# First MLP product of blocks 1 to 7 as seven quarter products, weight sums by adding DMAs

## The chip, the cores and the metric

One core of a Trainium2 chip. The time is that of the whole kernel on the device, in microseconds. Three runs of the kernel before took 737.86, 737.99 and 738.38 us; the median is 737.99.

## The reference, cut to what matters

The kernel computes one decoder layer on 512 tokens of 1024 channels, in float32. Two token mixers (a gated linear recurrence and a sparse attention) come first; the change leaves them alone. Then comes the MLP:

```python
        hm = rms_norm(x, mlp_norm_g[l])
        x = x + jnp.square(jax.nn.relu(hm @ w_mlp_in[l])) @ w_mlp_out[l]
    return rms_norm(x, final_norm_g)
```

`w_mlp_in` is 1024 x 4096, `w_mlp_out` 4096 x 1024.

## The kernel before, in words

**Three matmuls for one.** Every float32 operand is split into a rounded part (float32r, "hi") and the remainder ("lo"); a product is hi x hi + hi x lo + lo x hi (`three`, L1518 to L1522). So each weight slab of 128 x 1024 that a DMA loads from `slabs` is rounded by ScalarE (`whi`, four slots) and its remainder taken by VectorE (`wlo`, four slots). `hi_done` and `lo_done` count them.

**The MLP in eight blocks.** A block is 512 hidden features (`FB`). Its first product, `hidden` (L1780), makes four tiles of 128 features x 512 tokens in banks 0 to 3, each from one slab by 8 x 3 matmuls of 512 columns: 96 matmuls. ScalarE applies relu and squares them into `hv`. The second product multiplies `hv` (512 tokens x 512 features) with 512 x 1024 weights. In blocks 0 to 6 this is done by seven products of half the size in each of the three directions instead of eight (Winograd's form of Strassen's scheme): `PRODUCTS` (L69) gives their order, `block_` on TensorE (L1793) does them with 12 matmuls of 512 columns each, 84 in all. It needs sums of the four weight parts (`w_sum` on VectorE, L1375: four per block, from the arrived `br` slabs) and of the four activation parts (`s_sum`, L1383). A product is rounded on ScalarE (`a_hi`, `hi_out`), its remainders are taken on VectorE (`a_lo`, `lo_out`), and VectorE adds the finished product from its two banks to `acc` in SBUF (`gather`, L1394), except for two products that stay in banks 4 to 7 over all blocks (`KEPT`). Block 7, `last_`, does its second product plainly, with 96 matmuls, adds the `acc` slabs to `y` and ends with the last norm.

**What sets the order.** Nothing is scheduled: each engine has its own list, written out by hand (`block_` and `last_` of ScalarE L942, VectorE L1402, TensorE L1793; a hardware loop over the blocks), and waits on counted semaphores. `full[b]` counts what TensorE finished in bank b, `free[b]` what was read out of it. SP issues the loads (`load_out` L517 for the four `br` slabs, L540 for the next block's `raw` slabs), each when `lo_done` says that the slab before it is used. GpSimd does nothing in the loop. In the mixer part it issues 23 DMAs of another kind (`split_by_dma`, L644, L649): an SBUF slab added onto another, `accum_op=ALU.add`, which gives a `wlo` remainder without VectorE.

Of the kernel before, what the change touches and what calls it, by code (L numbers as in the profile page):

```python
# [18 lines left out]
F32 = mybir.dt.float32  # L19
# [49 lines left out]
PRODUCTS = (1, 7, 4, 5, 6, 3, 2)  # L69
# [5 lines left out]
def build(nc, x, slabs, vecs, consts, onehot, rel_bias, final_g, out):  # L75
    with ExitStack() as ctx:
# [6 lines left out]
        def sem(name):  # L83
# [92 lines left out]
        ssg, r2y = small[:, 242:246], small[:, 246:250]  # L176
# [10 lines left out]
        br_in = {k: sem(f"br_in{k}") for k in br}  # L187
        hi_done, lo_done, lod_done, slab_used = sem("hi_done"), sem("lo_done"), [sem(f"lod_done{q}") for q in range(SLOTS)], sem("slab_used")
# [11 lines left out]
                 "rik_done ry_done rf_done fe_done z_done act_fin pool_step acc_zero wt_done s_done ah_done al_done ymix_done mix_step iqh_done aqh_done kdh_done ikh_done ikl_done")  # L200
# [198 lines left out]
        NST = NFB - 1  # L399
        WPB = 4 + len(PRODUCTS)  # L400
        PBANKS = ((0, 1), (4, 5), (2, 3), (0, 1), (2, 3), (0, 1), (6, 7))
        KEPT = (1, 6)
        USE_B = [4, 4, 3, 3]

        def in_use(m, it):

            return it * USE_B[m] + MB

        def out_use(p, q, it):

            b = PBANKS[p][q]
            return it * USE_B[b] + (MB + {0: 1, 3: 2, 5: 3, 2: 1, 4: 2}[p])

        def product_full(p, q, it):

            b = PBANKS[p][q]
            return full[b], it + (MB2[b - 4] + 1) if p in KEPT else out_use(p, q, it) + 1

        def loop_blocks(eng, body, last):

            with eng.Fori(0, NST, 1) as it:
                body(it)
            last(NST)
# [39 lines left out]
        a_src = [a_part(0, 0), two(sa), a_part(1, 1), two(sb), two(sx), two(sa), a_part(0, 1)]  # L463
        w_src = [br["11"], br["12"], wt4, wt1, wt2, br["22"], br["21"]]
        w_last = [br["11"], br["21"], br["12"], br["22"]]
        w_last_in = ["11", "21", "12", "22"]
        hh3 = hh[:, :].rearrange("p (k t) -> p k t", k=4)
# [32 lines left out]
        def _(sp):  # L500
# [13 lines left out]
            def mlp_slab(m, it):  # L514
                return slabs[bass.ds(it * PER_FB + (NPLAN + m), 1), :, :].rearrange("a p c -> (a p) c")

            def load_out(it):  # L517

                for k, m, after in (("11", 4, WPB - 3), ("12", 6, WPB - 5), ("22", 7, WPB - 1), ("21", 5, WPB)):
                    sp.wait_ge(lo_done, it * WPB + (NLO - WPB + after))  # L520
                    sp.dma_start(br[k][:, :], mlp_slab(m, it)).then_inc(br_in[k], 16)
# [8 lines left out]
            sp.wait_ge(S["mxl_done"], KD_)  # L530
            sp.dma_start(fg[:, :], final_g.partition_broadcast(P)).then_inc(fg_in, 16)
# [1403 lines left out]
```

## Time and profile before

| | us |
|---|---|
| median of three runs | 737.99 |
| the profiled execution | 737.4 |
| its span | 735.7 |
| TensorE busy | 718.9 |
| VectorE busy | 513.0 |
| ScalarE busy | 378.4 |
| GpSimd busy | 109.2 |
| first matmul of the MLP starts, from the span's start | 399.4 |
| last matmul of the MLP starts | 728.4 |

The profile shows one execution. TensorE's row "busy" is the time in which at least one matmul is under way; matmuls overlap, so the number of them times the duration of one is more than that. "Idle before" in the table of groups is the time for which an engine stood still before such an instruction, with the work that released it.

### The profile page before, as it was taken

How to read it: one execution, taken by the hardware profiler on the slowest of the kernel's cores; microseconds unless marked ns; L12 is line 12 of the kernel's file. 1: busy time of each engine (PE TensorE's matmuls, PEld its weight loads, DVE VectorE, ACT ScalarE, POOL GpSimd, SP SyncE). 2: the span in 40 equal slices, each digit the busy share in tenths (PEclk: the TensorE clock that was granted, in tenths of full speed). 3: DMA queues.
4: the chain of work that ended last, by engine and by line, in shares of the span. 5: the costliest groups of instructions: out<-in, count | busy, mean ns of one | idle time of the engine just before them, and what ended most of it. 6: DMA issues, size and time to landing. Idle time of an engine off the chain costs nothing.

```text
span 735.7 us, 9813 instructions
## 1 busy us (share of the span) xinstructions
PE 718.9 (98%) x3490; PEld 603.1 (82%) x3490; DVE 513.0 (70%) x791; ACT 378.4 (51%) x595; POOL 109.2 (15%) x145
## 2 busy tenths in 40 slices
PE   5999999999999999999999999999999999999996
PEld 4788878888888888888888888888888888888885
DVE  5686996777896754337435695868778695968964
ACT  6463545867854665543224654545364544545432
POOL 4421241012212456400200100000000000000002
PEclk9999999999999999999999999999999999999999
DMA  8555123644997653112713242241515051332002
GB/s 298 153 99 150 58 90 83 132 117 105 224 221 176 144 119 110 58 58 86 257 58 129 101 142 87 88 141 57 171 36 190 2 171 57 116 113 86 30 1 114
DMA packets 25051, 85.12 MB, mean 116 GB/s; under 512 B 2712, under 2 KB 4920, under 8 KB 25016
## 3 DMA queue, kind: packets, MB, share of 16 engines
q1 hardware_dynamic: 19104, 67.87, 27.5%
q0 software_dynamic: 3312, 12.06, 8.8%
q10 hardware_dynamic: 2600, 4.72, 2.9%
q8 instruction: 22, 0.36, 0.2%
q14 instruction: 13, 0.11, 0.1%
HBM read 68.91 MB, written 3.67 MB: 99 GB/s over the span
## 4 chain that ended last, share of the span: by engine, by line
PE 95%; ACT 2%; DVE 1%; DMA 1%; issue 0%; POOL 0%; SPq 0%; POOLq 0%; DVEq 0%; ACTq 0%
PE bank L1520 20%; PE bank L1522 20%; PE bank L1521 20%; PE bank L1566 9%; PE bank L1570 8%; PE bank L1567 8%; PE bank L1751 2%; PE bank L1528 2%; PE bank L1659 2%; DMA xs<-x 1%; PE bank L1733 1%; PE bank L1732 1%; PE bank L1649 1%; PE bank L1650 1%; PE bank L1710 0%; PE bank L1671 0%
## 5 line engine op out<-in xcount | busy, mean ns | idle before, releaser
L1520 PE MATMUL bank<-hTh,whi 128*128 128x512 f32 (+1 forms) x264 | 102.8, 389 | 0.5 <-DVE hTl L1045 0.5
L1522 PE MATMUL bank<-hTh,wlo 128*128 128x512 f32 (+1 forms) x264 | 102.7, 389 | 0.0
L1521 PE MATMUL bank<-hTl,whi 128*128 128x512 f32 (+1 forms) x264 | 102.7, 389 | 0.0
L683 ACT CAST whi<-raw 128x1024 fp32r<-128x1024 f32 x58 | 60.3, 1041 | 41.3 <-PE bank L1522 40.7
L1566 PE MATMUL bank<-hTh,whi 128*128 128x512 f32 x192 | 78.0, 406 | 1.0 <-DVE hTl L1045 1.0
L1520 PE MATMUL bank<-whi,ah 128*128 128x512 f32 x196 | 76.2, 389 | 0.0
L1521 PE MATMUL bank<-wlo,ah 128*128 128x512 f32 x196 | 76.2, 389 | 0.0
L1522 PE MATMUL bank<-whi,al 128*128 128x512 f32 x196 | 76.2, 389 | 0.0
L1570 PE MATMUL bank<-hTl,whi 128*128 128x512 f32 x192 | 75.1, 391 | 0.0
L1567 PE MATMUL bank<-hTh,wlo 128*128 128x512 f32 x192 | 74.9, 390 | 0.0
L934 ACT ACTIVATE rt<-bank 128x512 f32<-128x512 f32 x32 | 19.1, 598 | 85.8 <-PE bank L1522 85.8
L1019 DVE TENSOR_TENSOR wlo<-raw,whi 128x1024 fp32r<-128x1024 f32 x34 | 45.3, 1334 | 24.6 <-ACT whi L683 24.6
L1520 PEld LDWEIGHTS bank<-hTh,whi 128*128 128x128 f32 (+1 forms) x264 | 49.2, 186 | 11.3 <-issue 0.7
L1521 PEld LDWEIGHTS bank<-hTl,whi 128*128 128x128 f32 (+1 forms) x264 | 49.2, 186 | 10.8
L1522 PEld LDWEIGHTS bank<-hTh,wlo 128*128 128x128 f32 (+1 forms) x264 | 49.2, 186 | 10.6
L925 ACT CAST whi<-raw 128x1024 fp32r<-128x1024 f32 x29 | 29.8, 1052 | 50.3 <-PE bank L1522 50.3
L1367 DVE TENSOR_TENSOR wlo<-br,whi 128x1024 fp32r<-128x1024 f32 x32 | 39.0, 1219 | 18.8 <-ACT whi L930 18.5
L666 POOL TENSOR_SCALAR small<-small 128x1 f32<-128x1 f32 x4 | 0.8, 191 | 310.0 <-ACT junk L702 310.0
L1400 DVE TENSOR_TENSOR acc<-bank,acc 128x512 f32<-128x512 f32 x70 | 44.8, 682 | 0.0
L1521 PEld LDWEIGHTS bank<-wlo,ah 128*128 128x128 f32 x196 | 36.8, 188 | 7.7
L1520 PEld LDWEIGHTS bank<-whi,ah 128*128 128x128 f32 x196 | 36.8, 188 | 7.6
L1522 PEld LDWEIGHTS bank<-whi,al 128*128 128x128 f32 x196 | 36.8, 188 | 7.6
(245 smaller groups left out, 1625.6 us busy)
## 6 DMA issues: line engine op xcount, KB each, us to landing
raw<-slabs SPq DMA_DIRECT2D x87, 512.0 KB, 3.5
br<-slabs SPq DMA_DIRECT2D x32, 512.0 KB, 3.5
wlo<-raw POOLq DMA_DIRECT2D x23, 512.0 KB, 4.9
xs<-x SPq DMA_DIRECT2D x4, 512.0 KB, 5.2
y<-x ACTq DMA_DIRECT2D x1, 2048.0 KB, 8.8
bias_rows<-rbias ACTq DMA_DIRECT2D x1, 1536.0 KB
out<-ys SPq DMA_DIRECT2D x3, 512.0 KB, 2.6
bt<-bias_rows ACTq DMA_DIRECT2D x1, 1024.0 KB, 6.1
```

What stands on the lines that cost most here:

```text
L683: act.copy(whi[s][:, :], raw[s][:, :]).then_inc(hi_done, 1)
L925: act.copy(whi[s][:, :], raw[s][:, :]).then_inc(hi_done, 1)
L934: act.activation(rt[m % 2][:, :], bank[m][:, :], ACT.Relu).then_inc(free[m], 1)
L1019: dve.tensor_tensor(wlo[s][:, :], raw[s][:, :], whi[s][:, :].bitcast(F32), ALU.subtract).then_inc(lo_done, 1)
L1367: dve.tensor_tensor(wlo[s][:, :], src[:, :], whi[s][:, :].bitcast(F32), ALU.subtract).then_inc(lo_done, 1)
L1400: dve.tensor_tensor(a_, bank[b][:, :], a_, ALU.add).then_inc(free[b], 1)
L1520: pe.matmul(dst, lh, rh, start=start, stop=False)
L1521: pe.matmul(dst, lh, rl, start=False, stop=False)
L1522: return pe.matmul(dst, ll, rh, start=False, stop=stop)
L1566: pe.matmul(dst, wh[:, k, c0:c0 + P], hi_[:, k, t0:T], start=k == 0, stop=False)
L1567: pe.matmul(dst, wl[:, k, c0:c0 + P], hi_[:, k, t0:T], start=False, stop=False)
L1570: ins = pe.matmul(dst, wh[:, k, c0:c0 + P], lo_[:, k, t0:T], start=False, stop=k == kt - 1)
```

## The change

It touches the MLP alone.

- The first product of blocks 1 to 7 (`up_product`, L2055) is done as the second one was: seven products over quarters, each 2 x 4 x 3 = 24 matmuls of 256 columns, 168 in all, in banks 3, 2, 3, 2, 3, 0, 3 (`UP_BANK`). Some products are added onto each other in the bank; ScalarE copies products 0, 1 and 2 out (`keep`), VectorE adds them onto products 3, 4 and 5 (`quadrant`), and ScalarE applies relu and the square by quadrant. Block 0 keeps the plain form. The activations' sums (T) are made once: GpSimd adds `hTh + hTl` in eight sums, VectorE makes four sums of 128x1024, ScalarE rounds four, VectorE takes four remainders, all during block 0.
- All weight sums, four for each product, are made by adding DMAs that GpSimd issues (`sums`), from slabs that SP loads: twelve loads a block instead of eight, seven of them (`load_quarter`) in two runs of 512 values per partition. VectorE's `w_sum` is gone.
- The second product has other signs, so that every weight sum is a plain addition, and three `ah` and `al` buffers in turn instead of seven. VectorE now takes 14 weight remainders a block, before 11. Block 0 copies its products to `acc`, where before GpSimd had set them to zero.

The core of the diff, from the file after. GpSimd:

```python
            def sums(it):

                pool.wait_ge(d1_in, it * 16 + 32)
                pool.wait_ge(br_in["22"], it * 16 + 32)
                add_into(d1, br["22"], ds_in[1])
                pool.wait_ge(br_in["12"], it * 16 + 32)
                pool.wait_ge(br_in["11"], it * 16 + 32)
                add_into(br["12"], br["11"], ds_in[3])
                pool.wait_ge(raw_in[ring(0)], raw_count(0, it + 1))
                pool.wait_ge(raw_in[ring(2)], raw_count(2, it + 1))
                add_into(r21, r11, us_in[3])
                pool.wait_ge(sl_in[1], it * 16 + 32)
                pool.wait_ge(raw_in[ring(3)], raw_count(3, it + 1))
                add_into(s1, r22, us_in[1])
                pool.wait_ge(lo_done, NLO + out_op(1, it))
                pool.wait_ge(ds_in[3], it * 16 + 32)
                pool.wait_ge(ds_in[1], it * 16 + 32)
                add_into(br["11"], d1, ds_in[2])
...
                pool.wait_ge(lo_done, NLO + out_op(3, it))
                pool.wait_ge(ds_in[2], it * 16 + 32)
                add_into(br["21"], br["11"], ds_in[4])
```

VectorE, the second half of a block:

```python
            def second_half(it):
                a_lo(3, it)
                lo_out(4, it)
                gather(1, it)
                lo_out(5, it)
                a_lo(4, it)
                gather(2, it)
                lo_out(6, it)
                a_lo(5, it)
                gather(3, it)
                a_lo(6, it)
                gather(4, it)
                lo_up(0, it + 1)
                gather(5, it)
                lo_up(1, it + 1)
                lo_up(2, it + 1)
```

ScalarE, the same half:

```python
            def second_half(it):
                ended(0, it)
                hi_out(4, it)
                a_hi(3, it, "hv_done", 4)
                ended(1, it)
                hi_out(5, it)
```

and SP, which loads the next block's slabs:

```python
            def next_out(it):

                sp.wait_ge(lo_done, NLO + out_op(1, it))
                load_out("12", 6, it + 1)
```

`hi_out(pos)` waits for the DMA or the sum whose slab it rounds: `ds_in[2]` for position 4, `ds_in[4]` for 6, `us_in` for quarter products 1 to 4.

The order of the instructions, on three engines. First VectorE, the second half of the MLP's loop before, from the sum for the fifth product on; `wlo`, `al` are remainders, L1400 is `gather`:

```order
L1392 TENSOR_TENSOR al_148<-sb,ah_141 128x512 [waits ah_done]
...
L1400 TENSOR_TENSOR acc_127<-bank,acc_127 128x512 [waits full0]
...
L1400 TENSOR_TENSOR acc_127<-bank,acc_127 128x512 [waits full1]
...
L1388 TENSOR_TENSOR sa<-hv,sx 128x512 [waits s_done,al_done]
...
L1392 TENSOR_TENSOR al_149<-sx,ah_142 128x512 [waits ah_done]
...
L1367 TENSOR_TENSOR wlo_60<-wt_133,whi_56 128x1024 [waits hi_done]
```

and in the file after, the same part of VectorE's loop (L1576 is the weight remainder, `d_133` the slab `d1`, `br_123` the slab `br11`, L1620 `gather`):

```order
L1589 TENSOR_TENSOR sx<-sb,hv 128x512 [waits s_done]
...
L1576 TENSOR_TENSOR wlo_58<-d_133,whi_54 128x1024 [waits hi_done]
...
L1599 TENSOR_TENSOR al_151<-sb,ah_148 128x512 [waits ah_done]
...
L1589 TENSOR_TENSOR sa<-sx,hv 128x512 [waits s_done,hv_done]
...
L1576 TENSOR_TENSOR wlo_59<-br_125,whi_55 128x1024 [waits hi_done]
...
L1599 TENSOR_TENSOR al_149<-hv,ah_146 128x512 [waits ah_done]
...
L1576 TENSOR_TENSOR wlo_60<-br_123,whi_56 128x1024 [waits hi_done]
...
L1620 TENSOR_TENSOR acc_127<-bank,acc_127 128x512 [waits full0]
```

Before, the first gather stood directly behind the remainders of position 3; now two weight remainders and an activation's stand between the last activation sum and it, and the last of them is that of `br11`.

GpSimd, from the start of the MLP on, in the file after (`hf_132` is hTh + hTl; the eight DMAs repeat for each block):

```order
L759 TENSOR_TENSOR hf_132<-hTh,hTl 128x2x256 [waits free3]
L666 TENSOR_SCALAR small<-small 128x4 [waits sq_done]
L667 TENSOR_TENSOR small<-small 128x4 [waits pool_step]
L765 TENSOR_TENSOR small<-small 128x4 [waits pool_step]
L766 TENSOR_SCALAR small<-small 128x4 [waits pool_step]
L769 DMA d_133<-br_126 128x1024 [waits br_in22,d1_in]
L769 DMA br_124<-br_123 128x1024 [waits br_in11,br_in12]
L769 DMA raw_50<-raw_52 128x1024 [waits raw_in1,raw_in3]
L769 DMA s_134<-raw_51 128x1024 [waits raw_in2,sl_in1]
L769 DMA br_123<-d_133 128x1024 [waits ds_in1,ds_in3,lo_done]
```

Before, GpSimd had five memsets and three small sums here and nothing in the loop.

ScalarE in block 0, in the file after (L1060 rounds a weight slab, L1087 a sum T, L1083 an activation):

```order
L1083 ACTIVATE ah_146<-hv 128x512 [waits hv_done]
L1060 CAST whi_53<-br_124 128x1024 [waits ds_in3]
L1087 ACTIVATE th_137<-hf_132 128x1024 [waits ts_done]
L1087 ACTIVATE th_138<-hf_132 128x1024 [waits ts_done]
L1087 ACTIVATE th_139<-hf_132 128x1024 [waits ts_done]
L1114 ACTIVATE rt_120<-bank 128x512 [waits full2]
L1116 ACTIVATE hv<-rt_120 128x512 [waits free2]
L1060 CAST whi_54<-d_133 128x1024 [waits ds_in1]
```

The relus of the third and fourth hidden tile, which before waited for their bank alone, now stand behind the rounding of `br_124` (`br12`), which waits for its adding DMA.

## Rows read from the trace of the kernel before

**Rows 1.** The page: busy us (share of the span) by engine; the chain that ended last

```profile
PE 718.9 (98%) x3490; PEld 603.1 (82%) x3490; DVE 513.0 (70%) x791; ACT 378.4 (51%) x595; POOL 109.2 (15%) x145
...
PE 95%; ACT 2%; DVE 1%; DMA 1%; issue 0%; POOL 0%; SPq 0%; POOLq 0%; DVEq 0%; ACTq 0%
```

**Rows 2.** Timeline of TensorE in the MLP: start us, us, engine, line, operation

```profile
455.05 0.39 PE L1522 MATMUL bank<-hTh,wlo 128*128 128x512 f32 x1
...
459.81 0.39 PE L1522 MATMUL bank<-hTh,wlo 128*128 128x512 f32 x1
```

**Rows 3.** Timeline of TensorE, the narrow products of the indexer

```profile
135.63 0.28 PE L1649 MATMUL bank<-ikh,iqs 128*128 128x256 f32 x1
...
136.11 0.40 PE L1520 MATMUL bank<-whi,hTh 128*128 128x512 f32 x1
```

**Rows 4.** Timeline around two 128-column products: weight loads and matmuls

```profile
233.48 0.19 PEld L1566 LDWEIGHTS bank<-oah,whi 128*128 128x128 f32 x1
...
233.59 0.19 PEld L1567 LDWEIGHTS bank<-oah,wlo 128*128 128x128 f32 x1
```

**Rows 5.** Groups of instructions, 480 to 680 us: busy us, mean ns, idle before

```profile
L1400 DVE TENSOR_TENSOR acc<-bank,acc 128x512 f32<-128x512 f32 x47 | 30.1, 682 | 0.0
...
L1367 DVE TENSOR_TENSOR wlo<-br,whi 128x1024 fp32r<-128x1024 f32 x20 | 24.4, 1219 | 15.5 <-ACT whi L930 15.5
...
L930 ACT CAST whi<-br 128x1024 fp32r<-128x1024 f32 x20 | 20.9, 1046 | 6.1 <-PE bank L1522 6.1
...
L936 ACT ACTIVATE hv<-rt 128x512 f32<-128x512 f32 x20 | 12.6, 632 | 0.6
L934 ACT ACTIVATE rt<-bank 128x512 f32<-128x512 f32 x20 | 12.0, 598 | 58.3 <-PE bank L1522 58.3
...
L940 ACT ACTIVATE ah<-hv 128x512 fp32r<-128x512 f32 x15 | 9.4, 625 | 0.0
L1392 DVE TENSOR_TENSOR al<-sa,ah 128x512 fp32r<-128x512 f32 x10 | 6.9, 688 | 8.2 <-ACT ah L940 8.2
```

**Rows 6.** Timeline of VectorE in one stretch without waits

```profile
469.19 0.68 DVE L1392 TENSOR_TENSOR al<-sx,ah 128x512 fp32r<-128x512 f32 x1
...
470.93 1.28 DVE L1400 TENSOR_TENSOR acc<-bank,acc 128x512 f32<-128x512 f32 x2
472.12 1.22 DVE L1367 TENSOR_TENSOR wlo<-br,whi 128x1024 fp32r<-128x1024 f32 x1
```

**Rows 7.** The adding DMAs of the mixer, issued at L649: time from issue to landing

```profile
DMA to landing us min/median/max: 4.5/4.9/8.0
```

**Rows 8.** The loads of the MLP, issued at L521: time from issue to landing

```profile
DMA to landing us min/median/max: 3.1/3.5/7.0
```

**Rows 9.** Windows: busy us of PE, PEld, DVE, ACT, POOL; PEclk, DMA share, GB/s

```profile
10.00:15.00 5.00, 4.02 (x26) 3.77 (x25) 4.10 (x7) 3.18 (x5) 1.46 (x3) 1.00 1.02 412
480.00:680.00 200.00, 200.00 (x884) 165.62 (x883) 148.20 (x176) 96.70 (x129) 0.00 (x0) 1.00 0.31 102
...
730.00:732.00 2.00, 0.00 (x0) 0.00 (x0) 1.56 (x3) 0.52 (x3) 1.23 (x2) 1.00 0.30 119
732.00:734.00 2.00, 0.00 (x0) 0.00 (x0) 0.58 (x1) 0.55 (x1) 0.00 (x0) 0.51 0.75 295
```

**Rows 10.** The page, DMA queues: packets, MB, share of 16 engines over the span

```profile
q0 software_dynamic: 3312, 12.06, 8.8%
```

**Rows 11.** GpSimd's small sums before the MLP, and its one wide sum

```profile
407.05 1.04 POOL L566 TENSOR_TENSOR small<-small 128x4 f32<-128x4 f32 x1
408.17 0.76 POOL L662 TENSOR_TENSOR small<-small 128x4 f32<-128x4 f32 x1
...
L580 POOL TENSOR_TENSOR wlo<-raw,whi x1: 2418/2418/2418, 16.3 to 16.3; 128x1024 fp32r<-128x1024 f32 x1
```

**Rows 12.** Timeline of TensorE where the MLP begins and where it ends

```profile
399.42 0.47 PE L1520 MATMUL bank<-hTh,whi 128*128 128x512 f32 x1 [0.52 <-DVE hTl L1045]
...
728.41 0.39 PE L1522 MATMUL bank<-whi,hl 128*128 128x512 f32 x1
```

More of the change, by code:

```diff
@@ L514, in mlp_slab @@
             def mlp_slab(m, it):
[L515 to L521, printed above, removed]
+                n = it * PER_FB + (NPLAN + PER_FB + m)
@@ L663, in _ @@
+            for it in range(-1, NST):
+                sums(it)
             for t in range(NT):
@@ new lines, in a_hi, with t_round, ended @@
+            def a_hi(pos, it, signal, val):
+                act.wait_ge(S[signal], it * 4 + (4 + val))
+                p = order(it)[pos]
+                act.activation(two(ah[pos % 3]), a_src[p], ACT.Copy, scale=SIGN_OF.get(p, 1.0)).then_inc(S["ah_done"], 1)
+            def t_round(i):
+                act.wait_ge(S["ts_done"], T_STEP[i])
+                act.activation(t_hi[i], t_src[i], ACT.Copy, scale=T_SIGN[i]).then_inc(S["thi_done"], 1)
+            def ended(pos, it):
+                act.wait_ge(*product_full(order(it)[pos], 1, it))
@@ new lines, in first_ @@
+            def first_():
+                act.wait_ge(full[7], MB2[3])
+                s = ring(3)
+                act.wait_ge(raw_in[s], 16 * ((NPLAN + 3) // SLOTS + 1))
+                round_(s, raw[s])
+                relu(0)
+                hi_out(0, -1)
+                relu(1)
+                a_hi(0, -1, "hv_done", 2)
+                hi_out(1, -1)
+                for i in range(3):
+                    t_round(i)
+                relu(2)
+                hi_out(2, -1)
+                relu(3)
+                a_hi(1, -1, "s_done", 1)
+                a_hi(2, -1, "s_done", 2)
+                hi_out(3, -1)
+                t_round(3)
+                second_half(-1)
@@ L1002, in _ @@
+            loop_blocks(act, first_, block_, last_)
             for t in range(NT):
@@ new lines, in out_product @@
+            def out_product(pos, it, begin, end):
+                p, s = order(it)[pos], ring(pos)
+                wh, wl = slab_view(whi, s, 2), slab_view(wlo, s, 2)
+                kept = p in KEPT
+                pe.wait_ge(lo_done, NLO + out_op(pos, it))
+                pe.wait_ge(S["al_done"], it * 7 + (7 + pos + 1))
+                for q in range(2):
+                    b = PBANKS[p][q]
+                    if not kept:
+                        pe.wait_ge(free[b], out_use(p, q, it))
+                    elif begin:
+                        pe.wait_ge(free[b], MB2[b - 4])
+                    for kk in range(2):
+                        ins = three(bank[b][:, :], two(ah[pos % 3])[:, kk, q * P:(q + 1) * P],
+                                    two(al[pos % 3])[:, kk, q * P:(q + 1) * P], wh[:, kk, :], wl[:, kk, :],
+                                    (begin or not kept) and kk == 0, (end or not kept) and kk == 1)
+                    ins.then_inc(full[b], 1)
@@ L1848, in _ @@
+            for m in range(4):
+                hidden(m)
+            for pos in range(7):
+                out_product(pos, -1, True, False)
+            with pe.Fori(0, NST - 1, 1) as it:
                 block_(it)
```

641 lines of the change are left out of this document (404 added, 237 removed).

## The prediction

> **What bounds the kernel now.** I read the page first. TensorE is busy for 98% of the span and holds 95% of the chain that ended last [rows 1]: a change pays where it shortens TensorE's work, and costs where it makes TensorE wait. Next the timeline: 21 matmuls of 512 columns start within 4.76 us, one per 0.2267 us [rows 2]. (The 0.39 us in a row is one matmul from start to end; they overlap, so the distance of starts is the price.) A block of the MLP is 96 + 84 of them, 40.8 us. The windows then say what is free: from 480 to 680 us TensorE never stops, VectorE is busy 148 of 200 us, ScalarE 97, GpSimd not at all, and the DMA engines 31% [rows 9]. VectorE is the one with little room.
>
> The profiled execution took 737.4 us (span 735.7, 1.7 around it), 0.6 less than the median 737.99. The sum is made against 737.4.
>
> **Part 1, the quarter products, seven blocks.** 96 matmuls of 512 columns become 168 of 256. The indexer has four such in a row, 0.48 us, so 0.120 each [rows 3]. Their weight loads last 0.19 us, but two loads without a wide matmul between them start 0.11 apart [rows 4]; that is under 0.120, so loads don't bind. 168 x 0.120 = 20.16 against 96 x 0.2267 = 21.76: 1.6 us less per block, **-11.2** for seven. (The Trainium skill, "TensorE: Matmul & The Clock Gate", section "Back-to-back issue gap", gives N / 2.4 + 2.5 ns, 216 and 109 ns, and 2.4 us less per block, -17 in all. The trace's starts are slower at both widths, so the rows are taken.)
>
> **Part 2, the middle of a block.** VectorE loses four weight sums and gets three more remainders and three quadrant sums, so its load hardly changes; but its work now comes late. Before, the operands of the second product grew from four hidden tiles spread over 21.8 us. Now the last three quadrants come out in the last 8.6 us of the first stage. Product 3 of the second stage writes banks 0 and 1, which `gather(1)` must have emptied, and this stands on VectorE behind `lo_out(4)`, for which ScalarE rounds the sum `br11 += d1` (`ds_in[2]`). That adding DMA may only be issued when `lo_out(1)` is done. I follow this chain from the end of quarter product 5 (t = 0):
> - ScalarE rounds ah0, then w11 (0.53 + 1.05); VectorE adds quadrant 5 and takes the remainder `lo_out(1)` (0.6 + 1.22) [rows 5]: done at 3.4.
> - The adding DMA lands 4.9 us after its issue [rows 7]. The load of `br12` starts on the same signal, on the same engines; a load holds them for 1.27 us (512 KB at the 412 GB/s of a full stretch [rows 9]) and lands 3.5 us after its issue [rows 8], so all of it falls into the adding DMA's time. 3.4 + 4.9 + 1.3 = 9.6.
> - Rounding (0.95), ah of product 3 (0.63), its remainder (0.60), `lo_out(4)` (1.14), half of `gather(1)` (0.68) [rows 5, 6]: 13.7.
> TensorE wants product 3 after quarter product 6 (24 x 0.120 = 2.9) and three second products of 12 x 0.2267 = 2.72: at 11.1. **It waits 2.6 us.** If the DMA were landed at once, VectorE's own queue would still be late: `lo_out(2)` can start at 6.3, and it, two remainders, a sum, two more wide remainders and half a gather are 5.9 us, so 12.2, a wait of 1.2.
> From there VectorE needs 2.93 us for each product (remainder, wide remainder, gather [rows 6]) and TensorE 2.72, so products 4 and 5 each start 0.2 late. Together 3.1 us a block in blocks 1 to 6: **+18.4**. The bounds of the wait are 1.2 (no DMA in it) and 4.7 (the longest landing, 8.0 instead of 6.2 [rows 7]); I take 2.6, since the median landing plus one load is the nearest row to what happens there.
>
> (The Trainium skill, "DMA: Bandwidth & Descriptors", "Anatomy of one DMA", fits a GpSimd-issued DMA as 2.0 us + bytes / 436e3, 3.2 us here; the trace's 4.9 contradicts it for adding ones.)
>
> **Part 3, block 0.** GpSimd must first form hTh + hTl in eight sums of 128x512, at half of 2.42 us each [rows 11], from where the MLP begins, 399.4 [rows 12]: 409. Behind them stand small sums (1.04, 0.76 and two short ones [rows 11]), and only then, at 411.5, the first adding DMA. `d1` and `br12` land one behind the other, beside the loads of `next_up`: the second at about 419 (4.9 + 2.8 + one or two loads). ScalarE waits there in `hi_out(1)`, and behind it stand three roundings of T, both last relus and squares, another cast: 7.6 us; then sum, rounding, remainder 2.0: 428.7. TensorE is due there at 399.4 + 21.8 + 2.7 = 423.9. So 4.8, plus 1.1 for product 3 by the same VectorE queue and 0.5 behind it: **+6.4**. The bounds are 2 and 10.
>
> **Part 4, the clock.** TensorE's granted clock stayed at full speed for at least 1.2 us after its last matmul (728.8) and had fallen to half, 1.2 GHz, in the window from 732 us, 3.2 us after it [rows 9, 12]. The waits of 2.6 us should not reach that, the one of 4.8 in block 0 can. No row shows how fast it comes back; nothing to +4, and I take **+1**.
>
> **The rest.** The twelve loads and eight adding DMAs of a block hold the engines for 12 x 1.27 + 8 x 2.8 (8.8% of 735.7 us for 23 of them [rows 10]) = 37.6 us of a block of 42.3: room, but little. VectorE's three sums and ten additions to y at the end, 3 x 1.14 and 10 x 0.6 = 9.4 us, lie beside 21.8 us of matmuls; I cost them at +0.3, since they stand ahead of the additions from the last banks. Memsets that go were idle time of GpSimd: nothing. Issues on SP cost 0.33 us each and SP is free.
>
> **Sum:** 737.4 - 11.2 + 18.4 + 6.4 + 1 + 0.3 = 752.3; **752.5** on the runs' level. A block takes 40.8 - 1.6 + 3.1 = 42.3 us.
>
> **The rivals.**
> - *The DMA engines are full* (chance 0.2). In the MLP of today eight loads per 40.8 us give the 31%, that is 1.58 us a load [rows 9], since the first packets from memory come slowly. At that price a block has 19 + 22.4 = 41.4 us of DMA, 98% of 42.3: the chains through `ds` and `us` then queue behind loads, and each block costs another 0.3 to 2 us, block 0 three more: 757 to 770, at 761 most likely. Against it: when the engines are really full they move a load in 1.27 us.
> - *Adding DMAs land early enough* (0.11). If landing takes 3 to 4 us in a queue that is warm, VectorE's queue alone sets the wait: 1.2 + 0.5 per block, +10, block 0 +5: about 742. The landing rows (4.5 at least, without a load beside it) speak against it. (The formula of the Trainium skill quoted above would give this case.)
> - *The faster side: TensorE does not wait in blocks 1 to 6* (0.04). It decides at product 3: the quadrants would have to be through ScalarE and VectorE 2.6 us sooner than by rows 5 and 6, or gather(1) be ready before. Then -11.2 + 6.4 stays: 733. For it: VectorE has a quarter of its time free. Against it: that time lies at the wrong end of the block; the point from which it is faster is a wait under 0.8 us a block, and even without any DMA I get 1.2.
> - *The narrow matmul is bound by its weight load* (0.02): at 0.19 us each, 168 cost 31.6 us, +10 a block, which would hide the waits: about 800. Rows 3 and 4 speak against it.
>
> **How the numbers follow.** The forecast (745 to 757) has 0.63. The range must leave out no more than 2 in 10: it goes from 743, most of the early-landing case, to 764, the better part of the full-engines case. A measurement of this kernel tells 0.2%, 1.5 us, from no change. Faster by more than that: the third rival and a rest, 0.05. Within it: 0.02, the piece between that and the early landings. Slower: 0.93.
>
> **What would show it.** TensorE's 256-column matmuls start 0.12 us apart (0.109 would be the formula, 0.19 the load). In blocks 1 to 6 TensorE has one idle piece of about 2.6 us, at the first matmul of product 3, put down to VectorE's gather, and two of 0.2 behind it; a block lasts 42.3 us. `br11 += d1` lands 6 us after its issue. In block 0 one piece of about 5 us before product 0, behind ScalarE's wait for `ds_in[3]`, and the clock perhaps at half after it. The DMA share in the loop is near 0.9. I am wrong if the block is under 41 us (then the chain through gather(1) is shorter than I count), or if the idle pieces lie in the first stage, before quarter products 3 or 4, where `s4` and `r21` are used: then the DMAs are too slow, not too late.

## The result and the profile after

| | before | after |
|---|---|---|
| median of 4 runs, us | 737.92 | **771.34** (767.43 to 772.44) |
| ratio, 95% interval | | 1.0442 [1.0402, 1.0482] |
| profiled execution / its span, us | 737.4 / 735.7 | 772.4 / 770.7 |
| TensorE busy | 98% | 94% |
| mean granted clock | 0.998 | 0.976 |

The change is slower, as forecast, but by 33 us and not by 15: outside the range of 743 to 764. The profiled execution is one of the two slowest of the four (both 772.44), so the ledger below explains 35 us.

The page of the changed kernel, the rows that answer to [rows 1] and [rows 10]:

```profile
PE 725.3 (94%) x3994; PEld 627.7 (81%) x3994; DVE 531.2 (69%) x814; ACT 414.6 (54%) x641; POOL 166.4 (22%) x205
PEclk9999999999999999999999899899999999999998
q0 software_dynamic: 11376, 41.42, 29.9%
PE 74%; ACT 7%; DMA 6%; DVE 5%; issue 4%; POOL 2%; DVEq 0%; POOLq 0%; ACTq 0%; SPq 0%
```

TensorE holds 74% of the chain instead of 95%; the rest now goes through ScalarE, a DMA and VectorE. The row PEclk has 8s inside the MLP, which the page of before did not have. The waits (window 400 to 735 us; columns: engine and line, what it waited for, us in total, times, longest):

```profile
PE bank L1782 <- DVE acc L1620: 18.6, 6, 3.3
PE bank L1782 <- issue: 6.1, 1, 6.1
ACT whi L1060 <- DMA br<-d: 14.9, 6, 2.7
```

The place is the forecast one: six waits for the gather, one per block, and one in block 0. They make 24.7 us. The one in block 0 stands before the block's second matmul product (product 1, counted from 0), the other six before product 3. Now the same wait in time order, TensorE in block 3, and what the clock did (windows of 1 us; the number after the five engines is the granted clock, then the DMA share and GB/s):

```profile
572.20 0.50 PE L1782 MATMUL bank<-whi,ah 128*128 128x512 f32 x1 [3.29 <-DVE acc L1620]
572.53 0.39 PE L1783 MATMUL bank<-wlo,ah 128*128 128x512 f32 x1
572.76 0.40 PE L1784 MATMUL bank<-whi,al 128*128 128x512 f32 x1
...
573.25 0.63 PE L1783 MATMUL bank<-wlo,ah 128*128 128x512 f32 x1
573.68 0.63 PE L1784 MATMUL bank<-whi,al 128*128 128x512 f32 x1
574.10 0.63 PE L1782 MATMUL bank<-whi,ah 128*128 128x512 f32 x1
```

```profile
572.00:573.00 1.00, 0.80 (x4) 0.67 (x4) 1.00 (x3) 0.00 (x0) 0.00 (x0) 1.00 0.90 164
573.00:574.00 1.00, 1.00 (x4) 0.84 (x3) 1.00 (x2) 0.70 (x1) 0.00 (x0) 0.59 1.02 197
574.00:575.00 1.00, 1.00 (x4) 0.71 (x4) 1.00 (x3) 0.88 (x2) 0.00 (x0) 0.50 1.06 197
575.00:576.00 1.00, 1.00 (x4) 0.81 (x3) 1.00 (x3) 0.00 (x0) 0.00 (x0) 0.50 0.98 217
576.00:577.00 1.00, 1.00 (x5) 0.79 (x4) 1.00 (x2) 0.16 (x1) 0.00 (x0) 0.70 1.03 401
577.00:578.00 1.00, 1.00 (x6) 0.81 (x5) 1.00 (x3) 0.47 (x1) 0.00 (x0) 1.00 0.98 381
```

TensorE restarts at 572.20 with starts 0.23 apart, and a microsecond later they are 0.43 apart: the granted clock has gone from 2.4 to 1.2 GHz, **after** the wait, while TensorE is fully busy again. The windows miss (0.41 + 0.50 + 0.50 + 0.30) = 1.7 us of full clock. So this wait costs 3.3 + 1.7. The profile does not put the second part down as a wait; it looks like work.

**The ledger.** The start of the first matmul of each stage cuts the MLP into pieces. The first stage of blocks 1 to 7 takes 20.15 us (forecast 20.16; before 21.76). The second stage takes 84 x 0.2267 = 19.04 us if nothing disturbs it; "end" is from the last matmul's start to the end of the span.

| us over before | forecast | measured |
|---|---|---|
| quarter products, 7 blocks | -11.2 | -11.3 |
| second stage of blocks 1 to 6 | +18.4 | +32.5 (25.6, 24.4, 24.4, 24.2, 23.9, 24.2 instead of 19.04) |
| block 0 | +6.4 | +9.1 (28.2 instead of 19.04) |
| clock | +1 | in the two rows above: 11.5 and 3.0 |
| end | +0.3 | +4.1 (11.4 instead of 7.3) |
| start of the MLP, 399.9 for 399.4 | 0 | +0.5 |
| sum | +14.9 | +34.9 |

The clock's share by the windows: half clock from 429.8 to 436.7 in block 0 (TensorE back at 430.75: 3.0 us lost), from 481.0 to 487.9 in block 1 (3.0), and 3.4 us in each of blocks 2 to 6 (1.7 each).

### The profile page after: what moved, and what is told of

The parts are those of the page before. It is cut to its first block, busy times and chain, and to the rows that moved or that the text cites. A ratio compares the mean times of both kernels' runs of the same rounds, so it can differ in the third digit from the quotient of the medians.

```text
span 770.7 us, 11238 instructions
## 1 busy us (share of the span) xinstructions
PE 725.3 (94%) x3994; PEld 627.7 (81%) x3994; DVE 531.2 (69%) x814; ACT 414.6 (54%) x641; POOL 166.4 (22%) x205
## 4 chain that ended last, share of the span: by engine, by line
PE 74%; ACT 7%; DMA 6%; DVE 5%; issue 4%; POOL 2%; DVEq 0%; POOLq 0%; ACTq 0%; SPq 0%
PE bank L1782 9%; PE bank L1784 9%; PE bank L1783 9%; PE bank L1828 8%; PE bank L1832 8%; PE bank L1829 8%; DMA br<-d 5%; PE bank L2070 4%; PE bank L2069 4%; PE bank L2067 4%; PE bank L2013 2%; PE bank L1790 2%; PE bank L1921 2%; DVE wlo L1576 1%; ACT whi L1060 1%
## 5 line engine op out<-in xcount | busy, mean ns | idle before, releaser
L1782 PE MATMUL bank<-whi,ah 128*128 128x512 f32 x196 | 83.5, 426 | 24.8 <-DVE acc L1620 18.6
L1060 ACT CAST whi<-br 128x1024 fp32r<-128x1024 f32 x46 | 47.8, 1041 | 45.7 <-DMA br<-br 21.4
L2070 PE MATMUL bank<-hTl,whi 128*128 128x256 f32 x224 | 63.4, 283 | 0.0
L2069 PE MATMUL bank<-hTh,wlo 128*128 128x256 f32 x224 | 63.4, 283 | 0.0
L2067 PE MATMUL bank<-hTh,whi 128*128 128x256 f32 x224 | 63.4, 283 | 0.0
L1229 DVE TENSOR_TENSOR wlo<-raw,whi 128x1024 fp32r<-128x1024 f32 x34 | 45.3, 1334 | 24.6 <-ACT whi L821 24.6
L1576 DVE TENSOR_TENSOR wlo<-br,whi 128x1024 fp32r<-128x1024 f32 x46 | 55.9, 1217 | 8.5 <-ACT whi L1060 8.5
L1576 DVE TENSOR_TENSOR wlo<-raw,whi 128x1024 fp32r<-128x1024 f32 x29 | 36.5, 1258 | 33.8 <-ACT whi L1060 33.8
L2067 PE MATMUL bank<-th,whi 128*128 128x256 f32 x168 | 47.5, 283 | 0.0
L2069 PE MATMUL bank<-th,wlo 128*128 128x256 f32 x168 | 47.5, 283 | 0.0
L2070 PE MATMUL bank<-tl,whi 128*128 128x256 f32 x168 | 47.5, 283 | 0.0
L2069 PEld LDWEIGHTS bank<-hTh,wlo 128*128 128x128 f32 x224 | 43.0, 192 | 0.3
L2067 PEld LDWEIGHTS bank<-hTh,whi 128*128 128x128 f32 x224 | 43.0, 192 | 0.3
```

Source lines behind the costliest of these rows:

```text
L1060: act.copy(whi[s][:, :], src[:, :]).then_inc(hi_done, 1)
L1576: dve.tensor_tensor(wlo[s][:, :], src[:, :], whi[s][:, :].bitcast(F32), ALU.subtract).then_inc(lo_done, 1)
L1782: pe.matmul(dst, lh, rh, start=start, stop=False)
L2067: pe.matmul(dst, wh[:, 4 * m + k, :], h_hi[q][:, k, :], start=m + k == 0 and not onto, stop=False, skip_group_check=True)
L2069: pe.matmul(dst, wl[:, 4 * m + k, :], h_hi[q][:, k, :], start=False, stop=False, skip_group_check=True)
L2070: ins = pe.matmul(dst, wh[:, 4 * m + k, :], h_lo[q][:, k, :], start=False, stop=k == 3, skip_group_check=True)
```

## The experiments

Theory T: waits on the chain of the adding DMA, VectorE's queue behind them, and a clock that falls behind a wait of 3 us; the end is VectorE's too. Its rivals stand with each run. All runs of the changed kernel stand in one table (the two staircases, which are made from the kernel before, follow below it), second stage by block and end, read from the traces as above:

| | us | ratio to before | block 0 | blocks 1 to 6 | end |
|---|---|---|---|---|---|
| the change | 771.3 | 1.0442 | 28.2 | 25.6 24.4 24.4 24.2 23.9 24.2 | 11.4 |
| TensorE kept busy | 762.1 | 1.0348 [1.0322, 1.0373] | 27.3 | 22.8 22.7 22.8 22.7 22.8 23.0 | 11.4 |
| small adding DMAs | 745.9 | 1.0115 [1.0098, 1.0132] | 22.5 | 21.0 21.0 21.0 21.0 21.0 21.1 | 11.4 |
| br12 late | 756.8 | 1.0266 [1.0249, 1.0283] | 27.6 | 21.9 22.0 21.9 22.0 21.8 21.8 | 11.4 |
| gather first | 756.6 | 1.0245 [1.0225, 1.0265] | 27.5 | 22.0 21.6 21.6 21.5 21.6 23.2 | 11.4 |
| early DMAs in block 0 | 768.0 | 1.0405 [1.0388, 1.0422] | 26.3 | 24.0 24.4 24.2 24.2 24.4 24.3 | 11.4 |
| br12 late, end reordered | 755.2 | 1.0233 [1.0216, 1.0250] | 28.2 | 22.0 21.8 21.8 21.9 21.9 22.0 | 9.3 |
| combined | 751.0 | 1.0172 [1.0156, 1.0187] | 25.1 | 23.5 21.7 21.5 21.5 21.5 21.5 | 9.3 |
| sums on GpSimd | 759.1 | 1.0294 [1.0279, 1.0310] | 24.0 | 23.0 22.4 22.5 23.3 22.9 23.0 | 9.3 |

### 1. What a wait costs: two staircases in the kernel before

In short (for the fine one each block has a single subtraction, of 433 to 968 columns of `cst`):

```diff
+ for it, widths in enumerate(((256,), (256, 128), (256, 256), ...)):     # GpSimd
+     pool.wait_ge(*product_full(2, 1, it))
+     for w in widths: pool.tensor_tensor(iks[:, 0:w], iks[:, 0:w], iks[:, 0:w], ALU.subtract)
  ...
+ if p == 3 and q == 0: pe.wait_ge(S["inj_done"], it + 1)                 # TensorE
```

> The kernel before with one wait more in each of blocks 0 to 6: TensorE waits ahead of product 3 for small subtractions on GpSimd (128x256, 0.85 us each, and 128x128, 0.65 us, by the rows of before), started when product 2 ends. Waits by that, with 0.3 us for the two signals and 0.1 for each link: 1.2, 1.9, 2.1, 2.9, 3.1, 3.8 and 5.0 us, 20 us together. Theory T (a wait of about 3 us or more costs a stretch at half clock behind it, one of about 2 does not): granted clock 1.00 behind the first three waits and at half for 3 to 7 us behind the last three, with the 2.9 open; time 738 + 20 + three to four times 1.7 to 3 us = 764 to 769. Rival (in the changed kernel the clock fell for another reason, such as narrow matmuls or the late second stage): no half clock here, every wait costs its length, 758. The one run also gives the price of each length of wait.

> The kernel before with one subtraction of GpSimd per block ahead of product 3 as in the first staircase, this time in finer steps: 433, 522, 612, 700, 790, 880 and 968 columns, each 0.4 us and 2.24 ns a column, 0.33 for the signals, waits of 1.7, 1.9, 2.1, 2.3, 2.5, 2.7 and 2.9 us. The first staircase kept full clock behind 1.33 and 1.68 and lost it behind 1.90. Theory T: half clock for about 3.4 us behind most waits from 1.9 on, 1.7 us each: 737.5 + 16.1 + 6 x 1.7 = 764. Rival (the fall behind 1.90 was by chance, the point is about 3 us): no fall, 753.6.

Measured 774.3 (1.0493 [1.0473, 1.0513]) for the coarse one and 758.5 (1.0280 [1.0259, 1.0300]) for the fine one. TensorE in the coarse run,

```profile
474.05 0.49 PE L1526 MATMUL bank<-whi,ah 128*128 128x512 f32 x1 [1.68 <-POOL iks L668]
517.04 0.49 PE L1526 MATMUL bank<-whi,ah 128*128 128x512 f32 x1 [1.90 <-POOL iks L668]
563.71 0.79 PE L1526 MATMUL bank<-whi,ah 128*128 128x512 f32 x1 [3.93 <-POOL iks L668]
```

and its row of the waits (us in total, times, longest):

```profile
PE bank L1526 <- POOL iks L668: 23.2, 7, 5.7
```

In the fine run TensorE behind three of the waits, and below it windows of 4 us:

```profile
516.82 0.49 PE L1526 MATMUL bank<-whi,ah 128*128 128x512 f32 x1 [1.80 <-POOL cst L668]
559.85 0.58 PE L1526 MATMUL bank<-whi,ah 128*128 128x512 f32 x1 [1.95 <-POOL cst L668]
649.50 0.49 PE L1526 MATMUL bank<-whi,ah 128*128 128x512 f32 x1 [2.25 <-POOL cst L668]
```

```profile
560.00:564.00 4.00, 4.00 (x11) 3.17 (x12) 2.13 (x3) 0.00 (x0) 0.00 (x0) 0.57 0.41 131
652.00:656.00 4.00, 4.00 (x20) 3.30 (x19) 3.44 (x5) 0.63 (x1) 0.00 (x0) 1.00 0.27 105
```

In the 4 us behind the wait of 1.95 us TensorE had 11 matmuls under way at a mean clock of 0.57, in the 4 us from 652 us, 2.5 us behind the restart after 2.25 us, 20 at full clock. All fourteen together: full clock behind 1.33, 1.66, 1.67, 1.68, 1.80 and 2.25; half clock behind 1.90, 1.95, 2.10, 2.53 (3.4 us of it) and 3.93, 4.14, 4.61, 5.65 (6.8 us). The coarse run took 36.8 us more for 23.2 us of waits, so 13.6 on top; the fine one 20.6 for 14.0. Not all of that is the clock: a second stage with a wait of 1.33 us lasts 1.6 us longer, one with 1.80 us 2.1, so each stop costs about 0.3 us besides its idle time, 2 us in each run. The clock has most of the rest. By block it is 1.6 us behind 1.90 and 2.5, 2.6, 2.4 and 1.7 us behind 3.93, 4.14, 4.61 and 5.65. This is the old kernel with its wide matmuls and its old VectorE queue: the fall needs none of the change, only the wait. Its point lies near 2 us, not at 3; between 1.9 and 2.3 both outcomes occur. The later runs add to this: full clock behind 2.04, 2.05 and 2.12 us, half behind 2.37 and behind every longer wait. The expected 764 of the fine run was too high for that reason (three falls instead of six), and because some waits came out shorter than set (14.0 us together instead of 16.1).

### 2. The change with TensorE kept busy

In short:

```diff
+ if pos == 3 and not begin:
+     for _ in range(12):
+         pe.matmul(bank[4][:, :], zero[:, 0:P], hTh3[:, 0, :], start=False, stop=False, ...)
```

> The changed kernel with 12 more 512-column matmuls on TensorE ahead of product 3 in blocks 1 to 6, with a stationary tile of zeros, added onto the kept bank 4 (the sum does not change). They last 12 x 0.2267 = 2.7 us and fill most of the wait of 3.1 to 3.3 us, so that TensorE hardly stops while everything else stays. Theory T (the clock falls because TensorE stood still for 3.3 us): wait left 0.3 to 0.6 us, granted clock 1.00 through the blocks 1 to 6, block 42.7 instead of 44.4 us, time 771.3 - 6 x 1.7 = 761, less still if the long half-clock stretch of block 1 goes. Rival A (the clock falls for another reason): half-clock stretches stay, 771. Rival B (the whole excess is a chain through VectorE and the DMA engines, the clock costs nothing on top because the engines behind set the pace): 771 as well, with the clock at 1.00.

Measured 762.1 beside 761 expected. One window of 250 us:

```profile
450.00:700.00 250.00, 249.15 (x1549) 220.91 (x1548) 181.68 (x219) 143.65 (x190) 39.58 (x46) 1.00 0.94 243
```

Clock at 1.00 and a second stage of 22.7 to 23.0 us, 1.6 less per block, though TensorE does 2.7 us **more** work there. Both rivals fall: adding work removed time, since the matmuls behind it ran at full clock. Two parts of the 9 us are not general: block 1 gives 2.8, since its fall had cost 3.0 us and not 1.7, and block 0, which the edit does not touch, gives 0.9 by a fall that came earlier.

### 3. The size of the adding DMAs

```diff
- pool.dma_start(to[:, :], of[:, :], accum_op=ALU.add).then_inc(signal, 16)
+ pool.dma_start(to[:, 0:8], of[:, 0:8], accum_op=ALU.add).then_inc(signal, 16)
```

> The changed kernel with each adding DMA cut to 8 of 1024 columns: the weight sums are left out (only their first 8 columns are formed), the order of issues and waits stays. This takes away the size of the adding DMAs, 30 of 37 per cent of the traffic and most of their landing time. Theory T: product 3 then waits only for VectorE's own queue, 1.2 us a block (as the prediction worked out), 0.2 to 0.5 behind it, no half clock; block 0 waits 1.5 to 2.5 us: 738 - 11.2 + 6 x 1.6 + 3 = 739, 737 to 742. Rival (VectorE's queue or the 256-column matmuls are the larger loss, the DMAs not): waits of 2.5 us and more stay at product 3, above 748.

The run leaves the weight sums out but for their first 8 columns, so its output is not the layer's; it serves for the time alone. Measured 745.9, above the 742 of T but far under the rival. TensorE in one block:

```profile
555.79 0.50 PE L1782 MATMUL bank<-whi,ah 128*128 128x512 f32 x1 [1.05 <-DVE acc L1620]
```

The wait of 1.05 is VectorE's own (forecast 1.2). The miss is the accounting: a block still loses 1.95 us and not 1.6, since the restarts and the small lags of products 4 and 5 come to 0.9, block 0 loses 3.5, and the end 4.1. That the end stayed at 11.4 us with the DMAs cut to a hundredth of their size showed that their traffic is not its cause.

### 4. The load beside the adding DMA

```diff
- sp.wait_ge(lo_done, NLO + out_op(1, it))
+ sp.wait_ge(ds_in[2], it * 16 + 32)
  load_out("12", 6, it + 1)
```

> The changed kernel with the load of br12 held back on SP until the adding DMA of ds_in[2] has landed, so that the two do not share the DMA engines. Theory T: br11 += d1 lands 4.9 to 5.3 us after its issue instead of 6.8, product 3 waits 1.6 to 2.0 us instead of 3.3, the clock stays at 1.00 in blocks 2 to 6, block 41.7 to 42.3 us instead of 44.4, time 755 to 759. Rival A (the landing is long by itself, or by the neighbours in GpSimd's queue): landing and wait stay, 770 or more, since the load comes later. Rival B (the clock falls for another reason than the wait): wait shorter but half-clock stretches stay, 761 to 763.

The chain in the change (block 3), then in this run:

```profile
561.21 0.35 SPq L571 DMA_DIRECT2D br<-slabs  x1
561.32 0.86 POOL L769 DMA_DIRECT2D br<-d  x1 [1.81 <-DVE wlo L1576]
568.11 1.05 ACT L1060 CAST whi<-br 128x1024 fp32r<-128x1024 f32 x1 [2.65 <-DMA br<-d]
569.71 0.69 DVE L1599 TENSOR_TENSOR al<-hv,ah 128x512 fp32r<-128x512 f32 x1 [2.14 <-ACT ah L1083]
570.32 1.22 DVE L1576 TENSOR_TENSOR wlo<-br,whi 128x1024 fp32r<-128x1024 f32 x1
571.46 1.28 DVE L1620 TENSOR_TENSOR acc<-bank,acc 128x512 f32<-128x512 f32 x2
```

```profile
554.34 0.86 POOL L769 DMA_DIRECT2D br<-d  x1 [4.51 <-DVE wlo L1576]
558.96 1.05 ACT L1060 CAST whi<-br 128x1024 fp32r<-128x1024 f32 x1 [0.48 <-DMA br<-d]
563.05 0.50 PE L1782 MATMUL bank<-whi,ah 128*128 128x512 f32 x1 [1.12 <-DVE acc L1620]
```

And a window of 200 us of it:

```profile
480.00:680.00 200.00, 192.03 (x1223) 170.99 (x1222) 148.04 (x179) 114.03 (x150) 31.03 (x36) 1.00 0.96 252
```

From the DMA's issue to the rounding of its sum 6.8 us with the load beside it, 4.6 without. One wait on the queue of loads, moved by a few microseconds, gives 14.5 us: the wait falls from 3.3 to 1.1, under the point where the clock falls. A second one of 0.6 to 0.8 us appears at product 5. There VectorE stood 0.8 us for the rounding of `br21 += br11`, the next adding DMA, so the landings still cost something. The DMA share is 0.96, against 0.93 in 480 to 680 us of the change: **the engines are nearly full in the faster variant too**, so a full share is not what makes the large loss; what stands beside the one DMA on the path is.

### 5. The order on ScalarE and VectorE

In short:

```diff
- a_lo(3, it); lo_out(4, it); gather(1, it); lo_out(5, it); a_lo(4, it)       # VectorE
+ a_lo(3, it); gather(1, it); lo_out(4, it); a_lo(4, it); lo_out(5, it)
- hi_out(4, it); a_hi(3, ...); ended(1, it); hi_out(5, it); a_hi(4, ...)      # ScalarE
+ a_hi(3, ...); hi_out(4, it); ended(1, it); a_hi(4, ...); hi_out(5, it)
```

> The changed kernel with two steps of the second stage swapped, on both engines: ScalarE rounds the operand of product 3 before the sum br11 + d1, and VectorE empties the banks of product 1 (gather(1)) before the remainder lo_out(4), which waits for that sum. Product 3 then needs nothing of the adding DMA; product 4 does, 12 matmuls later. Theory T: the wait of 3.3 us at product 3 becomes 0.7 to 1.2 us (VectorE's own queue, 1.05 in the run with the small adding DMAs), and one of 0.5 to 2 us comes at product 4, since landing (6.8) and cast stay; both under 1.7, so the granted clock stays at 1.00 from block 1 on; second stage 21.0 to 22.3 us instead of 24.3, time 771.3 - 6 x 2.3 - 3 = 752 to 760. Rival (the DMA chain as a whole sets the block, the order does not matter): the same 3.3 us come at product 4, time 768 and more.

Measured 756.6. Product 3 no longer waits; TensorE's wait now stands at product 4, and it is 1.1 us long:

```profile
566.65 0.47 PE L1782 MATMUL bank<-whi,ah 128*128 128x512 f32 x1 [1.15 <-DVE acc L1620]
```

Behind it come 0.3 to 0.5 us at product 5 in blocks 2 to 5 (0.8 in block 1; block 6 waits 2.05 and 1.1, which makes its 23.2 us). The wait has moved, as the rival said, but not with its 3.3 us. This run and the one before it end at 21.5 to 22 us a stage, by two links. The 1.1 us are VectorE's queue, which works without a gap from 557.7 us until product 4 has its banks; before that it stood 0.8 us for ScalarE's rounding of `d1`. In front of product 5 VectorE stands 0.5 us for the rounding of `br21 += br11`, which waits for its landing.

### 6. Block 0

In short:

```diff
  for k in MLP_K:
+     if k == MLP_K[4]: first_sums(-1)      # d1 += br22, br12 += br11
      ... pool.tensor_tensor(hf5 ...)
```

> The changed kernel with GpSimd's first two adding DMAs of block 0 moved ahead of four of its eight sums hTh + hTl and of its small sums. Theory T (block 0's wait of 6.1 us is the late issue, 413.9 us, of these two): they are issued some 9 us earlier (four sums of 1.25 us from 399.4), product 0 of block 0 waits 0 to 2 us instead of 6.1, the wait may come back at product 3 (3 to 4 us, with its own half clock), block 0's second stage takes 24 to 25.5 instead of 28.2 us; blocks 1 to 6 stay as they are (24 to 25 us). Time 771.3 - 3 = 767 to 769. Rival (ScalarE's queue of roundings makes the wait): 6.1 stays, no change of time.

The changed kernel's block 0, GpSimd, ScalarE and TensorE:

```profile
409.37 1.05 POOL L666 TENSOR_SCALAR small<-small 128x4 f32<-128x4 f32 x1
410.50 1.91 POOL L667 TENSOR_TENSOR small<-small 128x4 f32<-128x4 f32 x1
...
412.79 1.20 POOL L766 TENSOR_SCALAR small<-small 128x4 f32<-128x4 f32 x1
413.94 0.95 POOL L769 DMA_DIRECT2D d<-br  x1
...
421.40 1.05 ACT L1060 CAST whi<-br 128x1024 fp32r<-128x1024 f32 x1 [8.39 <-DMA br<-br]
...
430.75 0.77 PE L1782 MATMUL bank<-whi,ah 128*128 128x512 f32 x1 [6.11 <-issue]
```

Measured 768.0, inside the expected 767 to 769, though not for the expected reasons: block 0 gives 1.9 us and lasts 26.3 (expected 24 to 25.5), its wait falls from 6.1 to 3.2, more than the 0 to 2 expected, and 1.4 come back at product 3. Another 1.6 us come from block 1, whose fall of the clock this time costs 1.7 us and not 3.0; nothing in the edit aims at that. The change itself was measured from 767.4 to 772.4, so the gain in time is not clear of its spread; the shorter wait is what the run shows. The wait did not vanish, since the two DMAs, issued 9 us earlier with four of GpSimd's sums right behind them, landed 8.9 and 11.6 us after their issue instead of 4.8 and 6.8. The combined run below has the same (8.8 and 11.4). Why they take longer there is not shown.

### 7. The end

In short, and with the late load of `br12` from experiment 4:

```diff
  quadrant(3, 2, rt[1], it)
+ mix(acc[4], acc[4], acc[2], ALU.add, 1)
  ...
  h_lo_(2, 1, 1)
+ mix(acc[1], acc[1], acc[3], ALU.add, 1)
```

> The changed kernel with br12's late load (as in the third run) and, in the last block, two of VectorE's three sums of acc moved from behind the last remainder into gaps of its first half. Theory T (the end is VectorE's backlog: after the last matmul the changed kernel needs 11.4 us, the one before 7.3): each moved sum takes 1.2 us off, so 9.0 us from the last matmul to the end and 756.8 - 2.4 = 754.4. Rival (the tail is long for another reason, the store of the output or GpSimd's small sums): 11.4 stays, 756.8.

VectorE in the last block of the changed kernel, and below it SP's last issue of an output store, before (L549) and in the change (L650):

```profile
748.70 4.05 DVE L1692 SCALAR_TENSOR_TENSOR y<-acc,small,y 128x512 f32<-128x512 f32 x6
752.79 4.04 DVE L1692 SCALAR_TENSOR_TENSOR y<-bank,small,y 128x512 f32<-128x512 f32 x6
758.60 1.28 DVE L1570 SCALAR_TENSOR_TENSOR ys<-y,small,fg 128x1024 f32<-128x1024 f32 x1 [1.76 <-POOL small L810]
759.80 0.75 DVE L1692 SCALAR_TENSOR_TENSOR y<-bank,small,y 128x512 f32<-128x512 f32 x1
...
761.65 0.75 DVE L1692 SCALAR_TENSOR_TENSOR y<-bank,small,y 128x512 f32<-128x512 f32 x1
```

```profile
732.95 0.43 SPq L549 DMA_DIRECT2D out<-ys  x1
...
765.89 0.43 SPq L650 DMA_DIRECT2D out<-ys  x1
```

Before, VectorE took the last bank within 0.1 us of the last matmul's end. Here that matmul ends at 759.7 and VectorE comes to its bank at 761.65, because it had started on the banks late (752.8), then stood 1.76 us for GpSimd's small sum of the last norm, and each of the last banks brings a final product of 1.28 with it. With two sums moved VectorE takes the last bank within 0.1 us of the matmul's end again, the end is 9.3 us instead of 11.4 (expected 9.0), and the run 755.2 beside 756.8.

That is the whole of VectorE's part, 2.1 of the 4.1 us. The other 2.1 lie behind the output stores. From SP's last issue to the end of the span it is 2.7 us before and 4.8 in the change. The stores land 2.3 us after that issue in both; then the trace has only GpSimd's closing instruction, which ends at 770.5, and before it was done at 733.8, ahead of the store. The change and all eight variants of it have this piece, the one with small adding DMAs too; the two staircases do not. The change lets GpSimd issue 56 adding DMAs more, which may be the cause; no run here isolates it.

### 8. Together, and one step too far

> The edits that worked, together: product 3's operand and gather(1) ahead of the DMA's sum, the first two adding DMAs of block 0 ahead of four of the eight sums, GpSimd's small sums behind all adding DMAs of block 0, and two of VectorE's three last sums moved into its gaps (br12's load as in the change). Theory T, added up from the single runs: blocks 1 to 6 need 21.6 us for the second stage as in the run with the swapped order, block 0 some 24 us (the 26.3 of the run with the early DMAs less the half clock and the part of its wait that the small sums made), the end 9.3 us behind the last matmul: 737.9 - 11.3 + 6 x 2.6 + 5 + 2 = 749, 747 to 751. All waits under 1.9 us, granted clock 1.00 from block 1 on. Rival (the gains overlap, since a wait that is taken away comes back at the next product): above 753. Under 738 it would beat the kernel before; no theory gives that, since VectorE needs 2.93 us for each product of 2.72.

Measured 751.0, at the upper edge of the expected 747 to 751. The clock stayed up from block 1 on, as expected, but two waits were over 1.9 us: 4.1 in block 0, with half clock behind it, and 2.04 at product 4 of block 1. It is the best version of the change found, 20 us faster than the change and 13 slower than the kernel before. In the steady blocks 21.5 us are left where 19.04 would be undisturbed: 2.5 lost, more than the 1.6 that the quarter products give. Of these, 1.15 are the wait at product 4 and 0.4 the one at product 5, by the same two links as in experiment 5.

The last run takes two sums per block from VectorE, in short:

```diff
- s_sum(sx, ...); s_sum(sa, ...)                                  # VectorE
+ pool.tensor_tensor(two(sx), two(sb), a_part(1, 1), ALU.add)     # GpSimd
+ pool.tensor_tensor(two(sa), two(sx), a_part(0, 1), ALU.subtract)
```

> The combined kernel with two of VectorE's small sums per block (sx and the second sa, 0.6 us each at VectorE's pace) formed by GpSimd in blocks 1 to 6. If VectorE's queue alone sets the two waits that are left (1.1 at product 3, 0.4 behind it), 1.2 us of work less in front of gather(1) takes 0.6 to 1.1 us off each block: 742 to 746. If another link holds product 3 (the operand by ScalarE, or the landing of br11 + d1 at product 4), the waits move and the time stays within 2 us of the combined kernel's.

Measured 759.1: 8 us **slower** than the combined one, which neither case expected. GpSimd and VectorE in block 3:

```profile
555.96 2.07 POOL L799 TENSOR_TENSOR sa<-sx,hv 128x512 f32<-128x512 f32 x1
...
554.89 2.01 DVE L1589 TENSOR_TENSOR wlo<-d,whi 128x1024 fp32r<-128x1024 f32 x1 [1.39 <-ACT whi L1073]
556.83 1.75 DVE L1612 TENSOR_TENSOR al<-sb,ah 128x512 fp32r<-128x512 f32 x1
558.50 1.21 DVE L1589 TENSOR_TENSOR wlo<-br,whi 128x1024 fp32r<-128x1024 f32 x1
...
558.63 0.50 PE L1793 MATMUL bank<-whi,ah 128*128 128x512 f32 x1 [1.70 <-DVE al L1612]
```

While GpSimd computes, VectorE's remainder of 1.22 us takes 2.01 and one of 0.69 takes 1.75; the next one, when GpSimd is done, is back at 1.21. The relief of 1.2 us on VectorE costs it 1.9 in the same place, and TensorE now waits already at product 2. Half of the relief would have given nothing in any case. The first of the two sums stood in front of a wait for ScalarE's rounding of `d1`, and this wait grew from 0.79 us in the combined run to 1.39 in the row at 554.89.

## Why the prediction was right, and where it failed

- **Part 1 was exact.** 168 matmuls at 0.120 apart: 20.15 us per block for 20.16. The Trainium skill's formula ("TensorE: Matmul & The Clock Gate", "Back-to-back issue gap"; there it is the gap of an isolated matmul) would have given, as an estimate, 168 x 0.109 = 18.3; the trace does not agree with it, and the rows of before were the right source.
- **Part 2 had place and mechanism right, the size low.** Product 3 waits behind gather(1), `lo_out(4)` and the adding DMA. Forecast 13.7 us of chain, measured from quarter product 5's end 14.5 (landing 6.8 instead of 6.2); the wait 2.8 to 3.3 instead of 2.6. Without the clock blocks 1 to 6 lost 32.5 - 11.5 = 21.0 us against 18.4. The floor of 1.2 us from VectorE's queue alone was measured as 1.05, yet with 0.9 of restarts and lags behind it where I had put 0.4. (The six blocks at 3.1 us are 18.6, not the 18.4 of the sum; and 752.3 + 0.6 is 752.9, not 752.5. Neither matters here.)
- **Part 4 is the step that failed.** "The waits of 2.6 us should not reach that": the rows of before have the clock at 1.00 in the whole window from 730 to 732 us, so it was still up 3.2 us after the last matmul and fell directly behind that (my "at least 1.2 us" read the same rows too low). I took this one fall, at the end of the kernel, as the length of wait that brings the clock down. It is not: in the twelve traces of this case the clock falls between 2.0 and 5.3 us after the last matmul, so a single row says little, and in the middle of the kernel the staircases put the point near 2 us. I also priced the fall at +1 for block 0 alone; it is 1.7 us or 3.0 behind each wait, 14.5 in all. This term alone carries the result out of the range.
- **Part 3** forecast a wait of 4.8, it was 6.1: the small sums on GpSimd took 4.6 us instead of 2.5, so the first adding DMA went out at 413.9 and not at 411.5. The rest of that chain held within half a microsecond. (The sum names "one or two loads" but counts none, and rightly: the second DMA landed 7.4 us after the first issue, the sum has 7.5.) The 1.1 and 0.5 us at product 3 and behind it did not occur in block 0, presumably since VectorE caught up while product 1 waited; by its own sum this wait stands before product 1, and "before product 0" in the signs is a slip.
- **The end** was costed at +0.3 and is +4.1. I had laid VectorE's 9.4 us beside 21.8 us of matmuls and left out that the last four remainders and the additions from the banks want the same 21.8; the work fits by its sum, but it comes before the banks in the queue, and what is late there is not hidden by anything. That is 2.1 us, as experiment 7 shows. The other 2.1, from the last store to the end of GpSimd's list, had no term at all.
- **The rivals.** Full DMA engines were named as the likeliest way to 757 to 770. The time would nearly have fitted; the mechanism did not: no wait in the first stage, and a share of 0.96 at 21.9 us per second stage. Without the runs, 771 could have passed for this rival. The early landings (the Trainium skill, "DMA: Bandwidth & Descriptors", "Anatomy of one DMA", gives 3.2 us as an estimate) did not occur: 4.6 us without the load beside it, 6.8 with it. Narrow matmuls bound by their weights: no.
- **What would be wrong** if the block was over 42.3 us was not thought through: I had listed a block under 41. It was 44.4.

Still open: why 2.25 us of wait left the clock up in one block and 1.90 brought it down in another; why the first two adding DMAs of block 0 land so late when they are issued early; and what GpSimd's closing instruction spends its time on.

## What to carry to other kernels

A TensorE wait has a price besides its length. In a kernel that is bound by TensorE look at the granted clock behind each wait, not only at the row of waits: here waits up to 1.8 us cost their length and 0.3 us, waits from 1.9 to 2.3 in three cases of seven 1.7 us more, waits from 2.4 to 3.3 nearly always these 1.7 more, and longer ones 1.7 to 3 us more. So shortening a wait below that point, even by reordering or by filling it with zero products, pays more than its microseconds. When work moves from an engine to DMAs, ask at which point of the block the result is wanted and what else is issued on that same signal: the load of 512 KB beside the adding DMA cost 2.2 us of landing and, with the clock, 14.5 us of 771. And follow every engine's list to the very end of the program, where nothing covers it.

## What the runs showed of the hardware

- The clock falls **after** the wait: TensorE came back at 572.20 with full clock, and half clock was granted from 573.2 to 576.6. It can also fall before TensorE restarts. In all 29 half-clock stretches of the MLP's blocks, in ten traces, the length was 3.4 us where the fall came 0.2 us before the restart or later (waits of 1.90 to 3.32 us, and one of 4.14), and 6.8 us where it came 0.8 to 3.2 us before it (one wait of 3.27, all others of 3.9 us and more).
- GpSimd arithmetic on SBUF tiles slows VectorE: 1.22 became 2.01 us, 0.69 became 1.75, while GpSimd's own 128x512 sum took 2.07 instead of 1.25 in block 0. The combined run has it stronger: a remainder of VectorE took 6.2 us at 407.8, while GpSimd made four such sums. GpSimd's DMA issues alone did not (VectorE's remainders in the change stay at 1.22). The Trainium skill ("SBUF — State Buffer", "SBUF: two separate sides") says that VectorE with two operands in SBUF and GpSimd share a pair of ports and one of them blocks; these rows agree.
- An adding DMA of 512 KB was landed and its sum in use 4.6 us after its issue without a load beside it and 6.8 with one of the same size (another adding DMA is under way in both).
